# Three modulation tiles summed on VectorE earlier, and a fill on GpSimd later, in a hybrid diffusion transformer step

## What is computed

```
sh1, sc1, gt1, sh2, sc2, gt2 = split(silu(c) @ w_ada + b_ada, 6)   # for c_ctx and for c
h = rmsnorm(x, g_attn) * (1 + sc1) + sh1
qa, ka, va, qb, kb, vb, ga, gb = split(h @ w_in)      # q, k of both mixers get an RMS norm per head
ya = window_attention(rope(qa), rope(ka), va, cache_a_k, cache_a_v, sink_a)   # mixer A
yb = neighbourhood_attention(qb, kb, vb, cache_b_k, cache_b_v, rpb_b)         # mixer B
m  = (sigmoid(ga) * (ya @ w_out_a) + sigmoid(gb) * (yb @ w_out_b)) @ w_o
x  = x + gt1 * m
x  = x + gt2 * ((silu(h2 @ w_gate) * (h2 @ w_up)) @ w_down)   # h2 = rmsnorm(x, g_ffn) * (1 + sc2) + sh2
```

## Time and profile before

| | |
|---|---|
| median of 3 runs | 918.42 us (915.38 to 920.15) |
| the profiled execution | 915.14 us, of which the trace spans 913.3 us |
| busy: PE, DVE, ACT, POOL | 893.3, 708.4, 468.9, 121.2 us |
| projection of q, k, v on PE | 28 to 166 us |
| mixer A, mixer B | 166 to 252 us, 252 to 320 us |
| the 64 passes at L1418 | about 1.28 us each, from 68 to 311 us |
| L774, fill of `vbz` | 0.945 us, at 1.0 us |

### The profile page before, as it was taken

The page is one execution under the profiler, slowest core; times in us unless marked ns, Lnnn a source line. Parts: engine busy times, 40 slices in busy tenths (PEclk is TensorE's granted clock), DMA queues, the critical chain, the costliest instruction groups (busy, mean ns, idle before and its releaser), DMA issues. The chain is left out here.

```text
span 913.3 us, 16483 instructions
## 1 busy us (share of the span) xinstructions
PE 893.3 (98%) x6235; PEld 836.4 (92%) x6235; DVE 708.4 (78%) x1322; ACT 468.9 (51%) x966; POOL 121.2 (13%) x154
## 2 busy tenths in 40 slices
PE   7999999999999999999999999999999999999997
PEld 5689888778888899999999899999999999999987
DVE  3657898889688779875447868988678888777986
ACT  4763444666676733343236844555445556544543
POOL 0000000000000000000000032322333222333311
PEclk9999999999999999999999999999999999999999
DMA  9854343452345111125304378869998876999766
GB/s 365 348 190 167 139 151 116 150 156 71 128 129 184 57 60 48 52 88 230 115 25 163 115 152 189 191 147 197 206 205 199 184 179 161 208 204 189 174 152 135
DMA packets 51487, 144.26 MB, mean 158 GB/s; under 512 B 5968, under 2 KB 12368, under 8 KB 50128
## 3 DMA queue, kind: packets, MB, share of 16 engines
q1 hardware_dynamic: 31856, 101.33, 33.6%
q0 software_dynamic: 18832, 41.10, 24.0%
q10 hardware_dynamic: 720, 0.77, 0.3%
HBM read 120.64 MB, written 12.19 MB: 145 GB/s over the span
## 5 line engine op out<-in xcount | busy, mean ns | idle before, releaser
L1278 ACT ACTIVATE w_hi<-stage 128x512 fp32r<-128x512 f32 (+1 forms) x186 | 104.6, 607 | 69.4 <-DMA stage<-stage 49.0
L1946 DVE TENSOR_TENSOR w_lo<-stage,w_hi 128x512 fp32r<-128x512 f32 (+1 forms) x186 | 116.9, 668 | 27.8 <-ACT w_hi L1278 27.4
L2522 PE MATMUL ps<-m_hi,w_hi 128*128 128x320 f32 x304 | 93.9, 309 | 0.0
L2522 PE MATMUL ps<-m_lo,w_hi 128*128 128x320 f32 x304 | 93.9, 309 | 0.0
L2522 PE MATMUL ps<-m_hi,w_lo 128*128 128x320 f32 x304 | 93.9, 309 | 0.0
L2522 PE MATMUL ps<-h_hi,w_hi 128*128 128x320 f32 x272 | 84.0, 309 | 0.0
L2522 PE MATMUL ps<-h_lo,w_hi 128*128 128x320 f32 x272 | 84.0, 309 | 0.0
L2522 PE MATMUL ps<-h_hi,w_lo 128*128 128x320 f32 x272 | 84.0, 309 | 0.0
L2522 PE MATMUL ps<-y_hi,w_hi 128*128 128x320 f32 x264 | 81.9, 310 | 1.8 <-DVE w_lo L1946 0.8
L1371 DVE TENSOR_TENSOR w_lo<-stage,w_hi 128x1024 fp32r<-128x1024 f32 x47 | 57.3, 1222 | 33.8 <-ACT w_hi L858 33.4
L858 ACT ACTIVATE w_hi<-stage 128x1024 fp32r<-128x1024 f32 x47 | 49.5, 1061 | 64.2 <-PE ps L2205 36.8
(11 more groups left out here) (278 smaller groups left out, 2384.3 us busy)
## 6 DMA issues: line engine op xcount, KB each, us to landing
stage<-w_main SPq DMA_DIRECT2D x118, 512.0 KB, 4.1
x<-w_ada SPq DMA_DIRECT2D x23, 512.0 KB, 4.5
stage<-stage POOLq DMA_DIRECT2D x38, 256.0 KB, 4.7
qk<-w_ada SPq DMA_DIRECT2D x7, 1024.0 KB, 11.3
scr<-w_main POOLq DMA_DIRECT2D x28, 256.0 KB, 6.0
y_t<-scr POOLq DMA_DIRECT2D x22, 320.0 KB, 6.4
s_second<-w_main POOLq DMA_DIRECT2D x26, 256.0 KB, 6.2
stage<-w_main POOLq DMA_DIRECT2D x19, 256.0 KB, 6.8
```

Source lines behind the costliest of these rows:

```text
L1278: act.activation(w_hi[:, slot, at:at + job_half(j) * P], left_stage(op, j), ACT.Copy).then_inc(left_hi[op], 1)
L1946: dve.tensor_tensor(w_lo[:, slot, w], left_stage(op, j), w_hi[:, slot, w].bitcast(F32), ALU.subtract).then_inc(left_lo[op], 1)
L2522: ins = pe.matmul(ps[:, BANK_OF[op], 0:TH], wt[:, slot, w], right(op, part, j, k), start=k == 0 and n == 0, stop=k == half - 1 and n == 2)
```

## The change

Units 6, 7 and 8 of the projection get two tiles each instead of one, so that 19 tiles are summed there instead of 16, and mixer A sums four instead of seven. Mixer A's parts then fill the steps 1 to 8; steps 9 to 14 have none. The zeroing of `bb` stays in step 14, now under a number of its own. GpSimd's fill of `vbz` moves behind the two copies.

```
-ADA2_OF = [0, 0, 0, 1, 2, 1, 1, 1, 1, 0, 0, 2, 2, 0, 1, 2, 2, 0]
+ADA2_OF = [0, 0, 0, 1, 2, 1, 2, 2, 2, 0, 0, 2, 2, 0, 1, 2, 2, 0]
 ADA2_QKV = sum(ADA2_OF)
-ADA2_A = 7
+ADA2_A = 4
+BIAS_STEP = 14
@@ SyncE
-                if p == 2 * ADA2_A:
+                if p == BIAS_STEP:
                     sp.wait_ge(bb_zero, 1)
@@ GpSimd
-            nc.gpsimd.memset(vbz[0:64, :, :], 0.0).then_inc(pool_set, 1)
 
             pool.wait_ge(score_done, 2 * 10)
             pool.wait_ge(rope_done, 5)
             for v in range(2):
                 ins = nc.gpsimd.tensor_copy(cbc_late[v], cbc[:, v * D_MODEL:(v + 1) * D_MODEL])
             ins.then_inc(cbc_moved, 1)
+            nc.gpsimd.memset(vbz[0:64, :, :], 0.0).then_inc(pool_set, 1)
@@ VectorE
+                if p == BIAS_STEP:
+                    dve.wait_ge(cbc_moved, 1)
+                    dve.wait_ge(ada_dve, ADA2_LATE)
+                    dve.memset(bb[:, :, :, 0:128], 0.0).then_inc(bb_zero, 1)
                 if ada2_sum(p):
                     ada2_part(*ada2_sum(p))
-                    if ada2_sum(p) == (ADA2_LATE - 1, 1):
-                        dve.wait_ge(cbc_moved, 1)
-                        dve.wait_ge(ada_dve, ADA2_LATE)
-                        dve.memset(bb[:, :, :, 0:128], 0.0).then_inc(bb_zero, 1)
```

## The result

The changed kernel takes 919.23 us (median of 20 executions, 916.02 to 923.44), the one before beside it 915.16 us (20, 912.23 to 920.43). The ratio is 1.0042, with a 95% interval of 1.0024 to 1.0059: slower, by 3.8 us or 0.4%. That is clear of no change, less than the forecast's +5.2 us, and inside the 0.5% that was named as the bound. (The medians themselves differ by 4.1 us; 3.8 us is what the ratio gives.) The median before is 3.3 us lower here than the 918.42 us of three executions on which the forecast of 923.6 us stood; so in absolute time the forecast lies 4.4 us too high, of which 3.3 us are that starting point.

The account below looks back on a forecast made before the run. PE, busy 98% of the span, was taken as the bound. Wait 3.3, clock 2.2, mixer A -0.4 and fill 0.1 summed to +5.2 us on a median of 918.42: 923.6 us, range 918.0 to 927.0.

Parts of the forecast that it names:

- The lag of DVE and the wait: Projection: three extra tiles make DVE's scalings 5.9 us late; PE waits 2.9 us after unit 11, costing 3.3 us.
- the 0.74 us before 110.77: DVE idle time in the projection, claimed to be no reserve because the whole group moves with DVE.
- Nothing more lost in the projection: After unit 12's delay, at mixer B's k, DVE's remaining 2.6 us lag is used up in its waits before mixer A.
- The clock: TensorE's clock expected to halve behind the wait after unit 11: +2.2 us, between 1.7 and 3.4, zero if no fall.
- The 6.8 us at half read at 5.24 us: Stretch after an idle start where PE ran at half clock; gave the upper clock price, 3.4 us.
- The rows at 15.75 us: Start of program: clock halved behind 20 one-column matmuls, 1.7 us lost; taken as evidence for a fall.
- From the profiled execution to the median: Profiled execution, 915.14 us, placed 3.3 us below the median of 918.42 us; +5.2 us then gave 923.6 us.
- the longer fall: Rival: clock halves for longer, or again behind mixer B's k; 925.5 to 927 us; chance 0.09.
- Mixer A: Removing six passes from steps 9 to 14 returns only step 16's wait: -0.4 us, bounds 0 and -0.8.
- The rival that DVE sets the pace there: Mixer A steps 9 to 14: DVE is the bound, passes return up to 7.9 us; 916.0 us; chance 0.07.
- The fill: GpSimd's `vbz` fill behind its copies, beside a mask pass reading PSUM: +0.1 us, bounds 0 and 0.9.
- The rival that the clock stays: The wait after unit 11 comes but no half clock follows: +3.0 us, 921.4 us; chance 0.29.

Follow-up runs that it names:

- spread: Against the kernel before: 19 projection tiles, two each in iterations 3, 5 and 6; mixer A's passes in steps 1-4 and 9-12; late fill; 912.09 us, ratio 0.9959.
- sums_only: The changed kernel with GpSimd's fill of `vbz` left at the start; 918.80 us, ratio 1.0034 to the kernel before.
- filler: The changed kernel plus 11 dense, unused 512-column matmuls on TensorE behind unit 11, before the waiting transposes; 918.02 us, ratio 1.0026 to the kernel before.
- fill_again: Second run of the kernel before with only GpSimd's fill of `vbz` moved behind its two copies; 915.81 us, ratio 0.9986.
- spread_again: Second run: kernel before with two projection tiles each in iterations 3, 5, 6, mixer A's passes in steps 1-4 and 9-12, late fill; 911.55 us, ratio 0.9953.
- change_again: The changed kernel, unaltered, run again as yardstick; 919.17 us, ratio 1.0040 to the kernel before.

## Why the prediction was right or wrong, step by step

- **The lag of DVE and the wait: right.** Forecast 6.1 us late at the sums of squares, 5.9 at the scalings, 2.9 of wait, unit 12 late by 3.3; measured 6.0, 5.7, 2.56 and 3.2. Reading the 0.74 us before 110.77 as no reserve was what made it come out: as a reserve it would have given 0.7 us less. The wait was read 0.3 us too long, much as the lag was (0.1 to 0.2 us).
- **Nothing more lost in the projection: right.** From unit 12's late end on, the blocks keep their distances: unit 12 ended 7.63 us later in the trace of the change (136.17 against 128.54), and the transposes of mixer A's step 0 started 7.70 us later (177.98 against 170.28).
- **The clock: the step that failed in the change's cost.** I took 2.2 us, between 1.7 and 3.4, for a fall that I gave little more than an even chance, and then put the whole of it into the sum. Where it falls it costs 1.5 us, less than the 1.7 us that I took as the least for a fall, since part lies under the transposes; and it falls in part of the executions, so that the mean clock losses leave 0.8 ± 0.5 us for it. The 6.8 us at half read at 5.24 us come from a cold start; behind this wait the clock was at half for 3.4 us both times. The rows at 15.75 us showed a fall behind one-column matmuls and not behind a wait, so they bore less on it than I thought. With 0.8 in place of 2.2 the sum is +3.8 us, and measured were +3.8 (4.1 by the medians); with 0 to 1.5 it would be +3.0 to +4.5, so the close agreement is in part luck. An effect that comes in some executions should have gone into the sum as price times share.
- **From the profiled execution to the median: the larger part of the miss in absolute time.** I put the profiled execution 3.3 us below the kernel's median, by three executions with 918.42 us. Twenty have 915.16 us, and the profiled one, 915.14, is no lower. The sum on the profiled execution gave 920.3 us, 1.1 us above the 919.23 us measured; carried over to the median it gave 923.6 us, 4.4 us above. Three executions that scatter by 2.3 us each are not enough to place a change of 0.5%.
- **A slip in a rival.** By its own terms the longer fall starts at 918.42 + 3.3 + 3.4 = 925.1 us and not at 925.5; nothing else rests on it.
- **Mixer A: right, a little small.** -0.4 forecast, -0.6 measured, at the place that was named. The rival that DVE sets the pace there is refuted by the six unchanged steps.
- **The fill: right,** nothing that can be told, where I took 0.1 us. That the pass beside it would be a mask pass held in the change; in spread it is a division, and that one was slowed.
- **The rival that the clock stays** (+3.0 us) lies below the measured difference about as far as the forecast lies above it, and sums_only's trace is an execution of that kind. So a mixture of the two fits best. (In absolute time, 921.4 us, it too lies above the measured 919.23 us, by the starting point.) Since the forecast was put at +0.57% and the result is +0.42%, the chances leaned too much on "slower by over 0.5%"; and most of the rest stood on "within 0.5%", which hides that both of the likely cases were slower.

## What to carry to other kernels

Work moved to an engine's idle time costs nothing until its lag passes the slack of the next thing that someone waits for, and its full length from there on; so add up idle rows only up to that meeting point, and leave out those that move with the work. Taking work off an engine pays only in the steps in which someone waits for it, so look for those first: by the rows the three tiles that were taken out of steps 9 to 14 returned 0.6 us, and moving four passes from steps 5 to 8 to steps 9 to 12 returned 2.1 us more. Look also at what such a move puts beside what: the same division takes 0.88 or 2.31 us. An effect of the clock behind a wait belongs in a forecast as its price times how often it comes. And the time from which a forecast starts needs as many executions as the effect is small.

## What the hardware showed beyond that

TensorE's clock halves at places that depend on the execution. At the start, between 13 and 40 us, it stood at half for nothing at all (filler), 3.4 us (before), 7 us (fill_again), 10 us (spread_again) or 13.5 us (the change), though the kernels start alike but for the fill. The fill is not what does it: the 87 executions of the kernel before alone have mean clocks from 0.989 to 1.000. In two traces (filler and change_again) it fell at about 495 us, behind three waits of 0.3 to 0.5 us for VectorE's `h_lo` and `w_lo`, and in fill_again at about 512 us, among four more of 0.2 to 0.4 us for `h_lo`; the trace of before has the same waits and no fall. The two windows, before and then change_again:

```profile
490.00:500.00 10.00, 8.80 (x59) 7.98 (x57) 6.61 (x12) 4.15 (x8) 0.70 (x1) 1.00 0.60 237
```

```profile
490.00:500.00 10.00, 8.79 (x48) 8.00 (x46) 6.85 (x13) 5.31 (x9) 0.70 (x1) 0.83 0.49 187
```

Busy time is the same to 0.01 us, and one lost 1.7 us of clock. For a kernel whose changes are worth 0.1 to 0.5%, the mean clock of each execution is therefore the first thing to look at in a comparison, with the time after TensorE's last matmul left out where a trace allows it.
